# The splitting of streamed weights on GpSimd, in two and four parts instead of one

## The reference

```python
proj = rmsnorm(x) @ w_in                    # q, k, v, u, z
h = x + rmsnorm(concat(attn, sgu) @ w_out)
g, up = split(rmsnorm(h) @ w_gate_up)       # "gu1": 1024 -> 2 x 2816
h = h + rmsnorm((silu(g) * up) @ w_down)    # "down1"
h = h + sigmoid(h @ w_pe_gate + b) * (p @ w_pe_proj)
mod = silu(c) @ ada_w + ada_b               # the modulation: 12 x 1024 outputs
for each of two layers:
    h = rms_norm(x) * (1 + sc1) + sh1
    x = x + g1 * attention(h)               # stick-breaking, then sparse with top-k
    h = rms_norm(x) * (1 + sc2) + sh2
    x = x + g2 * conv_ffn(h)                # "gu2", "down2"; "gu3", "down3"
```

## Time and profile before

| | us |
|---|---|
| median of 3 runs | 1903.52 (1902.6 to 1904.52) |
| the profiled execution | 1902.92 |
| its span, from the first to the last instruction | 1901.1 |
| TensorE busy (9510 matmuls) | 1875.4 |
| weight loads of TensorE | 1535.5 |
| VectorE busy | 1081.1 |
| ScalarE busy | 524.7 |
| GpSimd busy (704 instructions) | 1210.0 |

### The profile page before, as it was taken

How to read it: one execution, slowest core, us unless ns; L and a number is a source line. 1 busy time by engine, 2 the same in 40 slices (tenths; PEclk the granted TensorE clock), 3 DMA queues, 4 the chain that set the end, 5 groups by cost and what they waited for, 6 DMA issues and landing times.

```text
span 1901.1 us, 27143 instructions
## 1 busy us (share of the span) xinstructions
PE 1875.4 (99%) x9510; PEld 1535.5 (81%) x9510; DVE 1081.1 (57%) x1690; ACT 524.7 (28%) x1091; POOL 1210.0 (64%) x704
## 2 busy tenths in 40 slices
PE   9999999999999999999999999999999999999999
PEld 7867778888888877779888888877777898888887
DVE  5966589998786515654533441144988463433322
ACT  4135300000115424442311221133368331112110
POOL 7641798887665564245766666655768657666673
PEclk9999999999999999999999999999999999999999
DMA  7530277776552231115333333223210223333331
GB/s 278 193 112 2 88 258 242 259 257 217 191 177 78 89 111 56 56 45 177 100 99 89 98 99 94 94 67 89 89 34 1 79 68 118 92 98 99 91 98 66
DMA packets 62325, 221.03 MB, mean 116 GB/s; under 512 B 6907, under 2 KB 7163, under 8 KB 62124
## 3 DMA queue, kind: packets, MB, share of 16 engines
q1 hardware_dynamic: 45216, 161.58, 27.5%
q10 hardware_dynamic: 17036, 58.46, 8.5%
HBM read 217.87 MB, written 2.14 MB: 116 GB/s over the span
## 4 chain that ended last, share of the span: by engine, by line
PE 93%; DVE 3%; POOL 1%; issue 1%; ACT 1%; DMA 0%; SPq 0%; DVEq 0%; POOLq 0%; ACTq 0%
PE bank L337 26%; PE bank L339 25%; PE bank L338 25%; PE bank L1027 1%; PE bank L1018 1%; PE bank L1156 1%; PE bank L1208 1%; PE bank L1199 1%; PE bank L372 1%; PE bank L468 1%; PE bank L472 1%; PE bank L469 1%; PE bank L373 1%; PE bank L377 1%; PE bank L762 1%
## 5 line engine op out<-in xcount | busy, mean ns | idle before, releaser
L1670 POOL TENSOR_TENSOR w_lo<-raw,w_hi 128x1024 fp32r<-128x1024 f32 x298 | 762.3, 2558 | 24.8
L337 PE MATMUL bank<-a_hi,w_hi 128*128 128x512 f32 (+1 forms) x2000 | 760.1, 380 | 2.4 <-DVE tmp L2477 1.6
L339 PE MATMUL bank<-a_hi,w_lo 128*128 128x512 f32 (+1 forms) x2000 | 758.4, 379 | 0.0
L338 PE MATMUL bank<-a_lo,w_hi 128*128 128x512 f32 (+1 forms) x2000 | 758.2, 379 | 0.0
L1668 POOL TENSOR_SCALAR w_hi<-raw 128x1024 fp32r<-128x1024 f32 x298 | 341.9, 1147 | 587.1 <-PE bank L339 453.0
L337 PEld LDWEIGHTS bank<-a_hi,w_hi 128*128 128x128 f32 x2000 | 376.4, 188 | 74.5 <-DVE tmp L2477 2.0
L339 PEld LDWEIGHTS bank<-a_hi,w_lo 128*128 128x128 f32 x2000 | 376.5, 188 | 70.8
L338 PEld LDWEIGHTS bank<-a_lo,w_hi 128*128 128x128 f32 x2000 | 376.6, 188 | 70.0
L2221 DVE CUSTOM_DVE_ANT_0 y<-y,cond 128x1024 f32<-128x1024 f32 x84 | 209.9, 2533 | 0.0
L2236 DVE SCALAR_TENSOR_TENSOR tmp<-bank,vecs,tmp 128x511 f32<-128x511 f32 x88 | 65.9, 749 | 240.9 <-ACT tmp L1944 240.8
L1944 ACT ACTIVATE tmp<-bank,vecs 128x512 f32<-128x512 f32 x88 | 68.2, 780 | 351.0 <-PE bank L339 347.1
(11 more groups left out here) (330 smaller groups left out, 2169.8 us busy)
## 6 DMA issues: line engine op xcount, KB each, us to landing
raw<-in_stream SPq DMA_DIRECT2D x299, 512.0 KB, 3.5
y<-in_ada ACTq DMA_DIRECT2D x96, 512.0 KB, 4.5
x<-in_x SPq DMA_DIRECT2D x4, 512.0 KB, 6.7
bias<-in_bias ACTq DMA_DIRECT2D x1, 2048.0 KB, 13.5
y<-rel_rows ACTq DMA_DIRECT2D x1, 2048.0 KB, 8.3
bias<-rel_rows ACTq DMA_DIRECT2D x1, 2048.0 KB, 13.2
out<-x SPq DMA_DIRECT2D x8, 256.0 KB, 2.0
cond<-in_c ACTq DMA_DIRECT2D x1, 512.0 KB, 6.9
```

The costliest lines, as they stand in the source:

```text
L337: pe.matmul(o, lhs_hi, rhs_hi, start=start, stop=False, **kw)
L338: pe.matmul(o, lhs_hi, rhs_lo, start=False, stop=False, **kw)
L339: return pe.matmul(o, lhs_lo, rhs_hi, start=False, stop=stop, **kw)
L1670: pool.tensor_tensor(w_lo[:, s, :], raw[:, j, :], f32(w_hi[:, s, :]), ALU.subtract).then_inc(split_ready, 1)
```

## The change

Each split of a 1024-wide block is issued in parts. The high part is made by two instructions of 512 columns and the low part by four of 256. Only the last part of each signals its semaphore, and the low parts still begin after the whole high part is complete. The code for the first block of the stream stays as it is.

```diff
@@ -1658,6 +1658,10 @@
         @block.gpsimd
         def _(pool):
+            def parts(n):
+
+                return [slice(p * (BLOCK // n), (p + 1) * (BLOCK // n)) for p in range(n)]
+
             def split(j, s, b, turn, wait=True):
                 pool.wait_ge(raw_landed[j], turn * 16 + 16)
                 if wait:
@@ -1665,9 +1669,13 @@
                     pool.wait_ge(block_done, b - (SPLIT - 1))
 
                 pool.sem_inc(split_begun, 1)
-                pool.tensor_scalar(w_hi[:, s, :], raw[:, j, :], 1.0, 1.0, ALU.mult, ALU.mult).then_inc(high_ready, 1)
+                for part in parts(2):
+                    m = pool.tensor_scalar(w_hi[:, s, part], raw[:, j, part], 1.0, 1.0, ALU.mult, ALU.mult)
+                m.then_inc(high_ready, 1)
                 pool.wait_ge(high_ready, b + 1)
-                pool.tensor_tensor(w_lo[:, s, :], raw[:, j, :], f32(w_hi[:, s, :]), ALU.subtract).then_inc(split_ready, 1)
+                for part in parts(4):
+                    m = pool.tensor_tensor(w_lo[:, s, part], raw[:, j, part], f32(w_hi[:, s, part]), ALU.subtract)
+                m.then_inc(split_ready, 1)
```

## The result

The changed kernel took 1929.97 us (median of 4 runs, 1929.76 to 1931.70); the kernel before, on the same chip, 1903.66. The ratio is 1.0141, its 95% interval 1.0129 to 1.0153: 26.3 us slower. Forecast were 1916.0 us, so +12.5. The sign was right and the time lies in the stated range, but the size was less than half of what came. Its profiled execution took 1929.92 us, span 1928.1, against 1902.92 and 1901.1: what follows explains these 27.0 us.

What follows compares the result with a forecast made beforehand. TensorE, busy 99%, was taken as the bound, with GpSimd and VectorE taking turns in gu1. Terms 8.0 + 0 + 3.4 + 0.6 + 0.5 + 0.5 - 0.5 = +12.5 us gave 1916.0 us, range 1904.5 to 1933.

Steps and rivals of the forecast that it cites:

- Price of a block: GpSimd's undisturbed split of one block: from 3.50 to 4.00 us, up 0.50; ends 3.80 and 4.35.
- down1 was put at 0: Down projection behind gu1: GpSimd needs 5.42 us a block against TensorE's 5.44, so 0 (0 to +4).
- gu1 was put at 8.0: gu1: two blocks need 11.3 us of GpSimd, 0.42 over TensorE's; 18 pairs lose 7.6, plus 2 at the start, less 1.56.
- At the start of gu1: Start of gu1: without lead, VectorE catches up sooner and GpSimd pays earlier: 2 us (0 to 5).
- The stall of the earlier trace: TensorE's wait for VectorE at 254.01, start of gu1: its 1.56 us go, as a column waits 0.5 us, not 2.3.
- out2, gu2 and gu3: Four splits in a row in out2 and before gu2 and gu3 end later, TensorE waits: +1.4, +1.0, +1.0.
- The first block: Start of the program: TensorE waits for a whole split, which grows, as VectorE's first splits step in: +0.6.
- the queries' scaling: Scaling of the first queries stands behind a split on GpSimd and TensorE waits for it: +0.5.
- The held port: Rival: GpSimd keeps the port through its parts, two places per block for VectorE; gu1 +3, about 1912 us; chance 0.12.
- The dearer part: Rival: 0.2 us or more per part, 4.35 us a block; gu1 +22, about 1937 us; chance 0.14.
- Faster: Rival: block stays at 3.50 to 3.65 us, gu1's wait goes, port waits shrink: about -2.5, 1901 us; chance 0.06.
- no change: Rival: block at 3.75 to 3.80 us, gu1 +1, the others +2, the lead swallows the rest: 1905 to 1907; chance 0.12.

Runs made afterwards that it cites:

- eighths: Against the kernel before: low part of each split in eighths of 128 columns, high part whole; 1971.84 us, 1.0361.
- tiny instructions: Against the kernel before: splits whole, four more GpSimd instructions of 8 columns into a scratch tile ahead of each high part; 1931.26 us, 1.0146.
- a whole gu1: Against the changed kernel: gu1's 44 blocks split whole, parts everywhere else; 1909.73 us, 1.0034 to the kernel before.
- a whole down1: Against the changed kernel: down1's 22 blocks split whole, parts everywhere else; 1923.44 us, 1.0104 to the kernel before.
- parts under cover: Against the kernel before: parts only in 108 blocks in steady stretches of gu2, down2, gu3 and down3, where GpSimd idled before each block; 1903.78 us, 1.0003.
- a sister kernel: Against the kernel before: low part of each split by quarters, high part whole; 1916.40 us, 1.0071.

## Why the prediction was half right

**Price of a block.** Forecast 4.00, measured 4.08: the mechanism was right, and the size as well, within 0.08. The halves of the high part were given 0.15 and cost it; the quarters were given 0.35 and cost 0.43. The 0.11 that the rows of 512 and 1024 gave is too little for a fixed share; by halves, quarters, eighths and tiny instructions it is 0.14 to 0.155. The Trainium skill (GPSIMD Engine Reference, section 3.1) led to an estimate of some 60 ns; every run here shows more than twice that, and the measurement decides.

Two steps failed: down1 was put at 0 and lost 8.2 us, because the sum left out with what lead the stage is entered; and gu1 was put at 8.0 and lost 12.4, with a pair of blocks sized at 0.42 us for 0.58 and its start at 2 us for 3.8. Together they are 12.6 of the 13.8 us by which the forecast was short.

**Gu1, +8.0 against +12.4.** The mechanism was right, and so was the number of pairs: seven periods of four blocks behind the first steady wait are 14, and the eight blocks up to it are 4 more. Their price was too small. The 0.08 that a block cost above the forecast counts twice in a pair and stands on a margin of 0.42: 0.58 a pair, 10.4 us for 18 pairs against 7.6. The other step that was mis-sized is "At the start of gu1 GpSimd has no lead and VectorE is behind by some turns; with six places per block to step in instead of two, VectorE catches up sooner and GpSimd pays earlier: 2 us (0 to 5)." The first eight blocks took 49.6 us instead of 43.5: 6.1 us, in waits of 0.72, 1.75, 1.56 and 0.89 and what follows them. At the steady price their four pairs make 2.3 of that, so the start itself cost 3.8 us and not 2. Without a lead each turn that VectorE catches up is TensorE's own loss; with VectorE's columns cut to 64 elements none of it is there. The stall of the earlier trace rows went as foreseen, worth 2.0 us with what follows it.

**Down1, 0 against +8.2.** This was the largest miss. "In the down projection behind it a block brings one column and one product: 4.00 + 0.95 + 0.47 = 5.42 against 5.44, so 0 (0 to +4)" compares two rates, and the rates were nearly right (5.50 against 5.44). It leaves out with what lead the stage is entered and what it asks for at its end. Here gu1, where GpSimd is saturated, hands down1 an empty buffer; at 5.50 us against 5.44 the lead is never won back, and the place where two splits are wanted at once costs the missing lead (2.50 us), and in this execution 1.7 us of clock behind it, which pe_proj gives back. The experiments show both halves: a whole gu1 sets down1 to 0, a whole down1 sets it to 1.2.

**Out1, 0 against +1.9.** Of the places with a row of splits I listed out2, gu2 and gu3, and left out the first one, eight in a row. What was late behind them was not TensorE's split alone but the sum of GpSimd that is queued behind it. Whole splits there removed it.

**The others.** Forecast +1.4, +1.0, +1.0 at out2, gu2 and gu3, measured +2.0, +1.4, +1.4: right places; with the price at 0.58 in place of 0.50 four splits end 0.3 later, which is most of the difference. The first block +1.0 for 0.6. Mix1 and qi +1.6 for 0.5: some of it goes with the clock. The granted clock was 0.51 from 1280 to 1290.5, and before 0.52 from 1256 to 1263.1. In the kernel with gu1 whole it was 0.50 for 6.8 us again, and this stretch lost 0.95; in the one with parts in gu1 alone it was low for some 10 us, and the stretch lost 0.6 with whole splits in it. The last attention gained 1.5 us where +0.5 had been set for the queries' scaling. That term had the wrong sign: it counted the longer splits ahead of the scaling and not that VectorE's part of the work comes earlier. Six kernels have the low part in quarters there, and in none does TensorE wait for the third scaling; with halves of the high part alone, and with parts under cover or in gu1 alone, the two waits of 0.34 us stay.

**The rivals.** The held port is refuted: VectorE's columns end after 1.68 us, one part of GpSimd between each two, though nothing signals between the parts. The Trainium skill (SBUF — State Buffer, section "SBUF: two separate sides") has the port given for a whole instruction; the trace agrees: a column waited for 2.3 us before and for 0.6 to 0.7 now. The dearer part (0.2 us or more) stood against 0.145 measured, but its time (1937) was closer than my forecast, for reasons of lead and not of price. "Faster" and "no change" needed a price of at most 0.15 and 0.30 us a block; it was 0.58. Halves of the high part alone cost 0.15, and that kernel does come out as the rival said, without loss. Of the signs that the prediction named, GpSimd's missing idle time in gu1, the columns (1.68 us for 1.6) and VectorE's idling came as said; the new wait came every fourth block with 0.9 us, not every second with 0.4.

## What to carry to other kernels

Cutting an instruction of GpSimd cost 0.14 to 0.155 us here for each further piece, at every width tried. It is free where the engine idles before each block; where it does not, TensorE loses what the engine's need exceeds its period by, so count that need stage by stage, with the turns of VectorE at the port in it. Then follow the lead: a stage that eats it passes the loss on to the next one, above all where that waits for two buffers at once. A wait of TensorE can cost again in its clock, and need not (1.7 us behind 2.50 us here, nothing behind 2.52 in a sister kernel), so look at the spacing of the matmuls behind it. And where a profile names a releaser, count which buffer it frees: here the one named was never awaited.

## What the runs showed of the hardware

- An elementwise instruction of 8 columns on GpSimd takes 0.155 us from start to start, so nearly all of it is fixed.
- Each column of VectorE (128x1024, two inputs in SBUF) took 0.98 us of GpSimd's time in the changed kernel (four quarters with two columns among them 4.79 us, 2.83 alone). A pair of blocks paid 3.27 to 3.32 us for three columns and a product, with low parts of 128 and of 256 columns; with a whole low part and tiny instructions it was 3.11.
- VectorE gets the port between two GpSimd instructions that neither wait nor signal: its columns ended every 1.68 us among parts of 256 columns.
- Behind 2.50 us of idling TensorE ran at 1.2 GHz for 3.4 us (matmuls 0.43 us apart); behind 2.52 us at the same place of another kernel the granted clock stayed at 1.00. Elsewhere it fell to that level during or behind 24 short matmuls of one column without such a wait, for 0, 3.4 or 6.8 us in the same place of three kernels; that stretch, of 55 us, took 1.6 us less with 0 and 1.4 more with 6.8 than with 3.4.
